# Decay and beta rows of a delta rule: by DMA broadcast from memory instead of by products with one-hot columns

## The chip, the cores and the metric

The kernel runs on one core of one Trainium2 chip. The metric is the time of one execution in device microseconds. Engines go by the names of the profile: PE (matrix products), DVE (vector), ACT (scalar, activations), POOL (GpSimd), SP (here only the issue of transfers). SBUF is the on-chip working memory of 128 partitions, PSUM the memory in eight banks that products are written to.

## The reference, cut to what matters

The program is two blocks, float32, for 512 tokens of width 1024. The first is a gated linear attention block with a routed mixture of experts. The second has a gated delta rule layer, a feed-forward layer, an attention layer and another feed-forward layer. The change lies in the gated delta rule, which for 8 heads of 128 computes

```
g_cum = cumsum(g within a chunk);  decay = exp(g_cum[i] - g_cum[j]) for i >= j
a_low = strict_lower((k*beta) @ k^T * decay)
[u, w] = solve(I + a_low, [v*beta, k*beta*exp(g_cum)])
attn  = (q @ k^T) * decay;   q_decay = q * exp(g_cum);   k_decay = k * exp(g_last - g_cum)
```

The kernel uses chunks of 128 tokens, so a head has four tiles of 128x128.

## The kernel before, in words

Stages follow each other, each in a block with a barrier of all engines at its end: the first block and its experts, then the projection stage of the delta rule, then the stage that inverts `I + a_low` (the one that changes), then the pass over the chunks with the output projection, a feed-forward, attention and a feed-forward.

In the projection stage ACT and DVE make `rows`, 8 partitions (one a head) by 4 rows of 512: row 0 is the decay's running sum, row 1 beta, row 2 a product of both, row 3 scratch. The same figures turned into columns are `gcols`.

The inverting stage goes over the heads in four pairs p (NPAIR), the two heads of a pair being u = 0 and 1. It needs row 0 and row 1 of each head repeated on all 128 partitions. `spread_rows` gets them by matrix products: the stationary operand is one column of the 8x8 identity repeated 128 times, the moving operand is `rows`, so that each product has 8 rows of contraction and 512 columns. The results are in PSUM banks 4u and 4u+1. From them:

- DVE `difference`: dm = (row 0 spread) - (column of the same), then the minimum of dm and 0
- ACT `exps`: er = exp(row 0 spread), then dm = exp(dm)
- DVE `decays`: dm times the triangular mask, then aT2 = (beta spread) * dm
- PE `pair_products` into the same two banks, once all of that has read them: K with K, Q with K; DVE `read_products` multiplies them by dm and aT2; `first_level` sets up the inverse tT2; `turn_t` and `turn_kv` transpose, ACT copies, DVE `keep_kd`.

Then a pair goes through six levels (LEVELS) of doubling. In each, POOL `mask` makes bmT from aT2, PE `level` multiplies it (L2006), ACT `keep_m` copies the result, PE multiplies twice more (L2006), and DVE `update` corrects tn and tT (L2238, L2240). After the sixth, `finish` applies the inverse.

Each engine's order is written out by hand: the preparation of pair p+1 stands at set places between the levels of pair p. On PE these are level 1: spread_rows, 3: pair_products, 4: turn_t, 5: turn_kv. On ACT 2: exps, 5: keep_t, 6: keep_kv. On DVE the differences stand ahead of the updates of level 2, `decays` behind the updates of levels 2 and 3, products and the first head's `first_level` ahead of the updates of level 4. Pair 0 has nothing beside it: its preparation is done in a row before the first level.

Weights come through `ring`, eight slots that SP fills (L203). In the inverting stage SP has no work.

Of the kernel before, what the change touches and what calls it, by code (L numbers as in the profile page):

```python
# [13 lines left out]
F32 = mybir.dt.float32  # L14
U8 = mybir.dt.uint8
F32R = mybir.dt.float32r
ALU = mybir.AluOpType
ACT = mybir.ActivationFunctionType
AX = mybir.AxisListType
P = 128  # L20
# [111 lines left out]
def program(nc, xT, ctxT, stream, experts, small, params, heads8, wdec, table, windows, outT):  # L132
    with ExitStack() as ctx:
# [13 lines left out]
        def sem(name):  # L147

            live.append(nc.alloc_semaphore(name))
            return live[-1]  # L150

        def kept_sem(name):
            return ctx.enter_context(nc.semaphore(name))
# [18 lines left out]

        h2_dram = nc.dram_tensor("h2_dram", (T, D), F32).ap()
        y_dram = nc.dram_tensor("y_dram", (2 * T, D), F32).ap()
        h_stored = kept_sem("h_stored")

        ident = tab[:, TABLES["ident"]]
# [185 lines left out]
        with nc.Block() as block:  # L363
            @block.sync
            def _(sp):
                load_blocks(sp, STREAM["out"].start + SLOTS)
# [1192 lines left out]
        rows = tab[0:8, TABLES["rcount"]].rearrange("p (a t) -> p a t", a=4)  # L1559
        ea = sb("ea", [8, 1], on=gdn)  # L1560
        ab_done, ab_act, ab_dve, ab_tr, ab_cols = (sem(n) for n in ("ab_done", "ab_act", "ab_dve", "ab_tr", "ab_cols"))
        st = gdn.enter_context(ExitStack())
        g_hi = sb("g_hi", [P, KT, T], F32R, on=st)
        g_lo = over("g_lo", [P, KT, T], F32R, "hn")
# [27 lines left out]
        with nc.Block() as block:  # L1592
# [144 lines left out]
            def _(act):  # L1737
# [48 lines left out]
                def step(ins):  # L1786
                    made[0] += 1
                    ins.then_inc(ab_act, 1)
                    act.wait_ge(ab_act, made[0])
# [4 lines left out]
                step(act.activation(rows[:, 3, :], rows[:, 3, :], ACT.Exp, scale=-1.0))  # L1794
                step(act.activation(rows[:, 3, :], rows[:, 3, :], ACT.Ln, bias=1.0))
                act.wait_ge(ab_dve, 5)
                step(act.activation(rows[:, 3, :], rows[:, 0, :], ACT.Exp))

                def roots(u, before):
# [162 lines left out]
        def tiles(x):  # L1962
            return x.rearrange("p (n i) -> p n i", n=TT)

        def every_tile(mask):
# [7 lines left out]
        tn2, tT2 = (sb(f"inv_{n}", [P, 2, 2, TT * H], on=st) for n in ("tn", "tT"))  # L1973
        er = sb("inv_er", [P, 2, T], on=st)
        whole = sml[:, 0:2 * T].rearrange("p (u t) -> p u t", u=2)
        names = ("spread", "diff", "expd", "exprow", "beta", "paired", "dve", "qdec", "t_tr", "kv_tr",
                 "t_copy", "kd_ready", "kv_ready", "masked", "m_done", "m_copy", "xy_done", "tn_up", "tT_up", "fin_done",
                 "fin_kept")
        S = {n: [sem(f"i_{n}{u}") for u in range(2)] for n in names}
# [10 lines left out]
        def off_block(x, rows):  # L1990
            return x[H * rows:H * rows + H, :].rearrange("p (n i) -> p n i", n=TT)[:, :, H:P]
        with nc.Block() as block:
            @block.tensor
            def _(pe):
                def four(out, lhsT, rhs):
# [11 lines left out]
                                          rhs[:, own if wide_rhs else near], start=True, stop=True)  # L2007
                    return m

                def spread_rows(p, u):  # L2010
                    h = 2 * p + u
                    if p:
                        pe.wait_ge(S["kd_ready"][u], p)
                        pe.wait_ge(S["kv_ready"][u], 2 * TT * p)
                    for a in range(2):
                        m = pe.matmul(ps[:, 4 * u + a, :], tab[0:8, h:h + 1].to_broadcast([8, P]), rows[:, a, :],
                                      start=True, stop=True)
                    m.then_inc(S["spread"][u], 1)

                def pair_products(p, u):  # L2020
                    h = 2 * p + u
                    pe.wait_ge(S["diff"][u], 2 * p + 1)
                    pe.wait_ge(S["exprow"][u], p + 1)
                    pe.wait_ge(S["beta"][u], p + 1)
                    four(ps[:, 4 * u, :], K[:, h, :], K[:, h, :])
                    four(ps[:, 4 * u + 1, :], K[:, h, :], Q[:, h, :]).then_inc(S["paired"][u], 1)

# [51 lines left out]
                    four(ps[:, 4 * u + 2, :], whole[:, u, :], V[:, h, :])  # L2079
                    four(ps[:, 4 * u + 3, :], K[:, h, :], whole[:, u, :]).then_inc(S["fin_done"][u], 1)  # L2080
                both = range(2)
                for part in (spread_rows, pair_products, turn_t, turn_kv):
                    for u in both:
                        part(0, u)
                for p in range(NPAIR):
                    beside = {1: spread_rows, 3: pair_products, 4: turn_t, 5: turn_kv} if p + 1 < NPAIR else {}
                    for lv in range(1, LEVELS + 1):
                        level(p, lv)
                        if lv in beside:
                            for u in both:  # L2090
                                beside[lv](p + 1, u)
                    for u in both:
                        finish(p, u)

            @block.scalar
            def _(act):
                def exps(p, u):
                    act.wait_ge(S["spread"][u], p + 1)
                    if p:
                        act.wait_ge(S["qdec"][u], p)  # L2100
                        act.wait_ge(S["dve"][u], DVES * p)
                    act.wait_ge(S["diff"][u], 2 * p + 1)
                    act.activation(er[:, u, :], ps[:, 4 * u, :], ACT.Exp).then_inc(S["exprow"][u], 1)
                    act.wait_ge(S["diff"][u], 2 * p + 2)
                    act.activation(dm[:, u, :], dm[:, u, :], ACT.Exp).then_inc(S["expd"][u], 1)

# [23 lines left out]
                def keep_result(p, u):  # L2130
                    h = 2 * p + u
                    act.wait_ge(S["fin_done"][u], p + 1)
                    for n, keep in enumerate((V, K)):
                        act.activation(keep[:, h, :], ps[:, 4 * u + 2 + n, :], ACT.Copy).then_inc(S["fin_kept"][u], 1)
                for part in (exps, keep_t, keep_kv):
                    for u in range(2):
                        part(0, u)
                for p in range(NPAIR):
                    beside = {2: exps, 5: keep_t, 6: keep_kv} if p + 1 < NPAIR else {}
                    for lv in range(1, LEVELS + 1):  # L2140
                        for u in range(2):
                            keep_m(p, lv, u)
                        if lv in beside:
                            for u in range(2):
                                beside[lv](p + 1, u)
                    for u in range(2):
                        keep_result(p, u)
# [32 lines left out]
            def _(ve):  # L2180
                def bycol(a, h):
                    return gcols[:, a, :, h:h + 1].to_broadcast([P, TT, P])

                def difference(p, u):
                    ve.wait_ge(S["spread"][u], p + 1)
                    ve.tensor_tensor(tiles(dm[:, u, :]), tiles(ps[:, 4 * u, :]), bycol(0, 2 * p + u), ALU.subtract
                                     ).then_inc(S["diff"][u], 1)
                    ve.wait_ge(S["diff"][u], 2 * p + 1)
                    ve.tensor_scalar(dm[:, u, :], dm[:, u, :], 0.0, None, ALU.min).then_inc(S["diff"][u], 1)

                def decays(p, u):
                    d = tiles(dm[:, u, :])
                    ve.wait_ge(S["expd"][u], p + 1)
                    ve.tensor_tensor(d, d, every_tile(tab[:, TABLES["incl"]]), ALU.mult).then_inc(S["dve"][u], 1)
                    ve.wait_ge(S["dve"][u], DVES * p + 1)
                    ve.tensor_tensor(aT2[p % 2][:, u, :], ps[:, 4 * u + 1, :], dm[:, u, :], ALU.mult
                                     ).then_inc(S["beta"][u], 1)

                def read_products(p, u):
# [887 lines left out]
```

## Time and profile before

| | |
|---|---|
| median of 3 runs | 2266.87 us |
| lowest and highest | 2261.90 and 2267.45 us |
| span of the profiled execution | 2263.8 us |
| mean granted TensorE clock | 0.939 of full speed |
| the inverting stage | from about 955.4 to 1131 us |

The profiled execution has no time of its own listed beside its span; the span lies within the three runs. The profile gives each instruction's place in that one execution, in microseconds from its start. The granted clock is the share of full speed at which PE was let run: 1.00 is 2.4 GHz, 0.50 is 1.2 GHz. A line number is that of the kernel; L2016 is the product of `spread_rows`, L1998 the product of `pair_products` (and of `finish`). PE counts each float32 product twice in the number of instructions.

### The profile page before, as it was taken

What the parts mean: (1) busy time and instruction counts of PE and PEld (TensorE: products, weight loads), DVE (VectorE), ACT (ScalarE), POOL (GpSimd) and SP (SyncE); (2) the same over time, 40 slices, a digit from 0 to 9 for tenths busy, and PEclk for the clock granted to TensorE, in tenths of its full rate; (3) what the DMA queues carried; (4) which work ended last, traced back from release to release, by engine and by line L of the source; (5) the groups of instructions that cost most, each with busy time, mean ns of one, the idle gap of its engine ahead of it and who ended that gap; (6) DMA issues with size and microseconds to landing.
All of it is one profiled execution on the core that took longest, in us unless ns stands there. A gap on an engine that the chain in (4) does not pass through costs nothing. (4 is left out here: it accounts for less than half of the span.)

```text
span 2263.8 us, 28841 instructions
## 1 busy us (share of the span) xinstructions
PE 2018.8 (89%) x11286; PEld 1512.0 (67%) x11286; DVE 994.9 (44%) x1397; ACT 688.1 (30%) x1078; POOL 321.3 (14%) x254
## 2 busy tenths in 40 slices
PE   5988884978785999678889999999999889999999
PEld 2756663322225777467887888888777677888887
DVE  3440444111115567855553444433488434434433
ACT  2432132111103445324432322222443543222222
POOL 1332010111113343033420100000100001000000
PEclk9999897999998999879989999999999889999999
DMA  8137016899981122100002222222222012222221
GB/s 340 47 131 269 12 63 252 330 423 425 423 344 76 68 91 84 56 2 2 3 10 78 100 93 93 102 93 103 77 82 75 10 38 84 93 102 93 96 100 47
DMA packets 61949, 283.32 MB, mean 125 GB/s; under 512 B 9984, under 2 KB 11296, under 8 KB 52512
## 3 DMA queue, kind: packets, MB, share of 16 engines
q1 hardware_dynamic: 53072, 266.95, 31.3%
q0 software_dynamic: 6256, 11.03, 1.3%
q10 hardware_dynamic: 2528, 4.01, 0.5%
q8 instruction: 69, 1.13, 0.2%
q14 instruction: 24, 0.20, 0.0%
HBM read 280.90 MB, written 14.68 MB: 131 GB/s over the span
## 5 line engine op out<-in xcount | busy, mean ns | idle before, releaser
L307 PE MATMUL ps<-ff_hhi,ff_whi 128*128 128x512 f32 x704 | 276.8, 393 | 8.6 <-DVE ff_hlo L2662 8.3
L308 PE MATMUL ps<-ff_hhi,ff_wlo 128*128 128x512 f32 x704 | 275.4, 391 | 0.0
L309 PE MATMUL ps<-ff_hlo,ff_whi 128*128 128x512 f32 x704 | 275.3, 391 | 0.0
L2580 DVE TENSOR_TENSOR ff_wlo<-ring,ff_whi 128x1024 fp32r<-128x1024 f32 x132 | 163.4, 1238 | 247.3 <-ACT ff_whi L2576 247.3
L2576 ACT ACTIVATE ff_whi<-ring 128x1024 fp32r<-128x1024 f32 x132 | 139.3, 1055 | 321.3 <-PE ps L309 299.7
L1451 PE MATMUL ps<-w_up,hgT 128*64 128x512 f32 x576 | 144.6, 654 | 45.8 <-DMA w_up<-experts 45.8
L307 PEld LDWEIGHTS ps<-ff_hhi,ff_whi 128*128 128x128 f32 x704 | 133.2, 189 | 38.5 <-DVE ff_wlo L2580 10.2
L309 PEld LDWEIGHTS ps<-ff_hlo,ff_whi 128*128 128x128 f32 x704 | 133.0, 189 | 28.0
L308 PEld LDWEIGHTS ps<-ff_hhi,ff_wlo 128*128 128x128 f32 x704 | 133.1, 189 | 27.7 <-issue 0.5
L307 PE MATMUL ps<-ff_ahi,ff_whi 128*128 128x512 f32 x352 | 136.9, 389 | 0.0
L308 PE MATMUL ps<-ff_ahi,ff_wlo 128*128 128x512 f32 x352 | 136.9, 389 | 0.0
L309 PE MATMUL ps<-ff_alo,ff_whi 128*128 128x512 f32 x352 | 136.9, 389 | 0.0
L1451 PEld LDWEIGHTS ps<-w_up,hgT 128*64 128x64 f32 x576 | 44.3, 150 | 133.9 <-issue 105.9
L307 PE MATMUL ps<-g_hi,g_w 128*128 128x512 f32 x256 | 103.2, 403 | 0.0
L309 PE MATMUL ps<-g_lo,g_w 128*128 128x512 f32 x256 | 102.2, 399 | 0.0
L308 PE MATMUL ps<-g_hi,ring_lo 128*128 128x512 f32 x256 | 100.3, 392 | 0.0
L1721 POOL TENSOR_TENSOR ring_lo<-ring,g_w 128x1024 fp32r<-128x1024 f32 x32 | 77.6, 2433 | 118.5 <-ACT g_w L1741 118.5
L2599 ACT ACTIVATE hctx<-hctx 128x512 f32<-128x512 f32 x44 | 27.8, 632 | 200.1 <-DVE hctx L2641 200.1
L309 PEld LDWEIGHTS ps<-ff_alo,ff_whi 128*128 128x128 f32 x352 | 66.1, 188 | 13.8
L308 PEld LDWEIGHTS ps<-ff_ahi,ff_wlo 128*128 128x128 f32 x352 | 66.1, 188 | 13.8
L307 PEld LDWEIGHTS ps<-ff_ahi,ff_whi 128*128 128x128 f32 x352 | 66.1, 188 | 13.5
L2641 DVE TENSOR_TENSOR hctx<-ps,ff_rs 128x512 f32<-128x512 f32 x44 | 30.4, 690 | 96.7 <-PE ps L309 96.7
(553 smaller groups left out, 3862.0 us busy)
## 6 DMA issues: line engine op xcount, KB each, us to landing
ring<-stream SPq DMA_DIRECT2D x276, 512.0 KB, 3.2
w_up<-experts SPq DMA_DIRECT2D x36, 2048.0 KB, 17.0
mix<-experts SPq DMA_DIRECT2D x18, 1024.0 KB, 20.8
hn<-experts SPq DMA_DIRECT2D x18, 1024.0 KB
yrow<-y_dram SPq DMA_DIRECT2D x4, 1024.0 KB, 8.0
tab<-table POOLq DMA_DIRECT2D x1, 2528.5 KB, 12.3
res<-xT ACTq DMA_DIRECT2D x1, 2048.0 KB
h_dram<-mix SPq DMA_DIRECT2D x4, 512.0 KB, 11.3
```

The source lines that it names most:

```text
L307: pe.matmul(out, w_hi, a_hi, start=start, stop=False)
L308: pe.matmul(out, w_lo, a_hi, start=False, stop=False)
L309: return pe.matmul(out, w_hi, a_lo, start=False, stop=stop)
L1451: m = pe.matmul(ps[half[u], s, :], hgT[:, s, k, half[u]], w_up[:, s, u, k * 512:(k + 1) * 512], start=k == 0, stop=k == KT - 1)
L1721: pool.tensor_tensor(ring_lo[:, s, :], ring[:, s, :], g_w[:, n % 4, :].bitcast(F32), ALU.subtract).then_inc(w_split, 1)
L2576: act.activation(w_hi[:, j % 2, :], ring[:, s, :], ACT.Copy).then_inc(w_rounded, 1)
L2580: ve.tensor_tensor(w_lo[:, j % 2, :], ring[:, (B0 + j) % SLOTS, :], w_hi[:, j % 2, :].bitcast(F32), ALU.subtract).then_inc(blocks_done, 1)
L2599: act.activation(sg[:, p % 4, :], sg[:, p % 4, :], ACT.Silu).then_inc(silu_done, 1)
L2641: ve.tensor_tensor(sg[:, p % 4, :], ps[:, 2 * (p % 4), :], rs[:, :], ALU.mult).then_inc(g_scaled, 1)
```

## The change

The two rows go to memory once and come back on all partitions by DMA.

- In the projection stage ACT issues one transfer of rows 0 and 1 of all heads to `rows_dram` (32 KB), between two of its steps.
- In the inverting stage SP issues for each pair two transfers of row 0 (one a head, 512 numbers read onto each of 128 partitions, 256 KB written) into dm, and two of row 1 into aT2. For pairs after the first the transfers into dm wait for `keep_kd` of the pair before (semaphore kd_ready) and its `dve` steps, those into aT2, from the third pair on, for the last mask of two pairs before.
- `spread_rows` is gone from PE: 16 products. `pair_products` no longer waits for the readers of the spread rows, only, from the second pair on, for the pair before.
- ACT makes er in a part of its own, `exp_rows`, from dm in SBUF; it stands one level earlier (1), `exps` of dm stays at level 2.
- DVE `difference` reads dm and writes dm, after er has been made; the beta product reads aT2 and writes aT2. Before, one operand of each was in PSUM.

```
+        rows_dram = nc.dram_tensor("rows_dram", (2, HEADS, T), F32).ap()
...
                 act.wait_ge(ab_dve, 5)
+                act.dma_start(rows_dram.rearrange("a h t -> h a t"), rows[:, 0:2, :]).then_inc(rows_out, 16)
                 step(act.activation(rows[:, 3, :], rows[:, 0, :], ACT.Exp))
...
+            @block.sync
+            def _(sp):
+                def all_rows(a, h):
+                    return rows_dram[a, h:h + 1, :].to_broadcast([P, T])
+                sp.wait_ge(rows_out, 16)
+                for p in range(NPAIR):
+                    for u in range(2):
+                        h = 2 * p + u
+                        if p:
+                            sp.wait_ge(S["kd_ready"][u], p)
+                            sp.wait_ge(S["dve"][u], DVES * p)
+                        sp.dma_start(dm[:, u, :], all_rows(0, h)).then_inc(S["g_in"][u], 16)
+                    for u in range(2):
+                        h = 2 * p + u
+                        if p >= 2:
+                            sp.wait_ge(S["masked"][u], LEVELS * (p - 1))
+                        sp.dma_start(aT2[p % 2][:, u, :], all_rows(1, h)).then_inc(S["beta_in"][u], 16)
...
-                def spread_rows(p, u):
+                def pair_products(p, u):
                     h = 2 * p + u
                     if p:
                         pe.wait_ge(S["kd_ready"][u], p)
                         pe.wait_ge(S["kv_ready"][u], 2 * TT * p)
-                    for a in range(2):
-                        m = pe.matmul(ps[:, 4 * u + a, :], tab[0:8, h:h + 1].to_broadcast([8, P]), rows[:, a, :],
-                                      start=True, stop=True)
-                    m.then_inc(S["spread"][u], 1)
-
-                def pair_products(p, u):
-                    h = 2 * p + u
-                    pe.wait_ge(S["diff"][u], 2 * p + 1)
-                    pe.wait_ge(S["exprow"][u], p + 1)
-                    pe.wait_ge(S["beta"][u], p + 1)
...
-                    beside = {1: spread_rows, 3: pair_products, 4: turn_t, 5: turn_kv} if p + 1 < NPAIR else {}
+                    beside = {3: pair_products, 4: turn_t, 5: turn_kv} if p + 1 < NPAIR else {}
...
-                def exps(p, u):
-                    act.wait_ge(S["spread"][u], p + 1)
+                def exp_rows(p, u):
+                    act.wait_ge(S["g_in"][u], 16 * (p + 1))
...
-                    act.wait_ge(S["diff"][u], 2 * p + 1)
-                    act.activation(er[:, u, :], ps[:, 4 * u, :], ACT.Exp).then_inc(S["exprow"][u], 1)
+                    act.activation(er[:, u, :], dm[:, u, :], ACT.Exp).then_inc(S["exprow"][u], 1)
+
+                def exps(p, u):
...
-                    beside = {2: exps, 5: keep_t, 6: keep_kv} if p + 1 < NPAIR else {}
+                    beside = {1: exp_rows, 2: exps, 5: keep_t, 6: keep_kv} if p + 1 < NPAIR else {}
...
-                    ve.wait_ge(S["spread"][u], p + 1)
-                    ve.tensor_tensor(tiles(dm[:, u, :]), tiles(ps[:, 4 * u, :]), bycol(0, 2 * p + u), ALU.subtract
+                    ve.wait_ge(S["exprow"][u], p + 1)
+                    ve.tensor_tensor(tiles(dm[:, u, :]), tiles(dm[:, u, :]), bycol(0, 2 * p + u), ALU.subtract
...
-                    ve.tensor_tensor(aT2[p % 2][:, u, :], ps[:, 4 * u + 1, :], dm[:, u, :], ALU.mult
+                    ve.wait_ge(S["beta_in"][u], 16 * (p + 1))
+                    ve.tensor_tensor(aT2[p % 2][:, u, :], aT2[p % 2][:, u, :], dm[:, u, :], ALU.mult
```

## Rows read from the trace of the kernel before

**Rows 1.** The page: busy time of the engines over the whole span.

```profile
PE 2018.8 (89%) x11286; PEld 1512.0 (67%) x11286; DVE 994.9 (44%) x1397; ACT 688.1 (30%) x1078; POOL 321.3 (14%) x254
```

**Rows 2.** Windows: length, busy PE, PEld, DVE, ACT, POOL, granted clock, DMA share, GB/s.

```profile
1034.70:1041.20 6.50, 6.47 (x96) 5.06 (x96) 1.96 (x5) 3.63 (x8) 2.14 (x2) 0.50 0.01 3
1107.00:1127.00 20.00, 18.22 (x512) 16.87 (x512) 8.78 (x23) 9.12 (x24) 10.69 (x10) 1.00 0.02 3
```

**Rows 3.** Timeline of pair 0's preparation: start, length, what.

```profile
955.44 7.16 PE L2016 MATMUL ps<-tab 8*128 8x512 f32 x8 [17.53 <-PEq L1592]
959.30 0.69 DVE L2186 TENSOR_TENSOR inv_dm<-ps,gcols 128x512 f32<-128x512 f32 x1 [1.63 <-PE ps L2016]
960.08 1.28 ACT L2103 ACT_TABLE_LOAD   x1 [12.47 <-DVE inv_dm L2186]
965.26 2.05 PE L1998 MATMUL ps<-K 128*128 128x128 f32 x8 [2.66 <-DVE inv_aT L2196]
972.41 1.64 DVE L2213 TENSOR_TENSOR inv_tT<-inv_aT,tab 64x256 f32<-64x256 f32 x2
```

**Rows 4.** Timeline of DVE: first update of levels 1, 2, 4 of pairs 0 to 2; 1, 2 of pair 3.

```profile
988.81 0.42 DVE L2238 TENSOR_TENSOR inv_tn<-inv_tn,ps 128x256 f32<-128x256 f32 x1 [4.57 <-PE ps L2006]
...
998.28 0.42 DVE L2238 TENSOR_TENSOR inv_tn<-inv_tn,ps 128x256 f32<-128x256 f32 x1 [2.77 <-PE ps L2006]
...
1010.62 0.42 DVE L2238 TENSOR_TENSOR inv_tn<-inv_tn,ps 128x256 f32<-128x256 f32 x1 [0.47 <-PE ps L2006]
...
1030.76 0.42 DVE L2238 TENSOR_TENSOR inv_tn<-inv_tn,ps 128x256 f32<-128x256 f32 x1 [6.34 <-PE ps L2006]
...
1039.95 0.42 DVE L2238 TENSOR_TENSOR inv_tn<-inv_tn,ps 128x256 f32<-128x256 f32 x1 [2.76 <-PE ps L2006]
...
1051.98 0.42 DVE L2238 TENSOR_TENSOR inv_tn<-inv_tn,ps 128x256 f32<-128x256 f32 x1 [0.47 <-PE ps L2006]
...
1071.10 0.42 DVE L2238 TENSOR_TENSOR inv_tn<-inv_tn,ps 128x256 f32<-128x256 f32 x1 [6.34 <-PE ps L2006]
...
1079.39 0.42 DVE L2238 TENSOR_TENSOR inv_tn<-inv_tn,ps 128x256 f32<-128x256 f32 x1 [2.48 <-PE ps L2006]
...
1090.72 0.42 DVE L2238 TENSOR_TENSOR inv_tn<-inv_tn,ps 128x256 f32<-128x256 f32 x1 [0.47 <-PE ps L2006]
...
1109.85 0.42 DVE L2238 TENSOR_TENSOR inv_tn<-inv_tn,ps 128x256 f32<-128x256 f32 x1 [6.34 <-PE ps L2006]
...
1113.32 0.42 DVE L2238 TENSOR_TENSOR inv_tn<-inv_tn,ps 128x256 f32<-128x256 f32 x1 [1.75 <-PE ps L2006]
```

**Rows 5.** Timeline of PE: spread products beside level 1 of pairs 1 and 2.

```profile
1031.62 4.38 PE L2016 MATMUL ps<-tab 8*128 8x512 f32 x8
...
1071.96 3.77 PE L2016 MATMUL ps<-tab 8*128 8x512 f32 x8
```

**Rows 6.** One line's instructions (min/median/max ns) and, last, POOL's mask in pair 3.

```profile
L2194 DVE TENSOR_TENSOR inv_dm<-inv_dm,tab x8: 681/685/1489, 963.7 to 1084.4; 128x512 f32<-128x512 f32 x8
L2196 DVE TENSOR_TENSOR inv_aT<-ps,inv_dm x4: 690/690/692, 964.4 to 1046.4; 128x512 f32<-128x512 f32 x4
L2163 POOL TENSOR_TENSOR inv_bmT<-inv_aT,tab x24: 1088/1094/1552, 970.4 to 1096.5; 128x512 f32<-128x512 f32 x24
1111.33 2.14 POOL L2163 TENSOR_TENSOR inv_bmT<-hctx,tab 128x512 f32<-128x512 f32 x2 [1.33 <-PE ps L2006]
```

**Rows 7.** The page: transfers by line, KB each, median us from issue to landing.

```profile
ring<-stream SPq DMA_DIRECT2D x276, 512.0 KB, 3.2
...
yrow<-y_dram SPq DMA_DIRECT2D x4, 1024.0 KB, 8.0
...
outT<-res SPq DMA_DIRECT2D x8, 256.0 KB, 2.1
```

**Rows 8.** Timeline: the last KD of pair 1 (DVE), then the last copy of its level 1 (ACT).

```profile
1023.75 0.67 DVE L2226 TENSOR_TENSOR KD<-ps,inv_dm 128x512 f32<-128x512 f32 x1
...
1029.70 0.78 ACT L2127 ACTIVATE inv_m<-ps 64x256 f32<-64x256 f32 x2 [0.19 <-PE ps L2006]
```

More of the change, by code:

```diff
@@ L1561, in program @@
         ab_done, ab_act, ab_dve, ab_tr, ab_cols = (sem(n) for n in ("ab_done", "ab_act", "ab_dve", "ab_tr", "ab_cols"))
+        rows_out = sem("rows_out")
         st = gdn.enter_context(ExitStack())
@@ L1975, in program @@
         whole = sml[:, 0:2 * T].rearrange("p (u t) -> p u t", u=2)
-        names = ("spread", "diff", "expd", "exprow", "beta", "paired", "dve", "qdec", "t_tr", "kv_tr",
+        names = ("g_in", "beta_in", "diff", "expd", "exprow", "beta", "paired", "dve", "qdec", "t_tr", "kv_tr",
                  "t_copy", "kd_ready", "kv_ready", "masked", "m_done", "m_copy", "xy_done", "tn_up", "tT_up", "fin_done",
@@ L2081, in _ @@
                 both = range(2)
-                for part in (spread_rows, pair_products, turn_t, turn_kv):
+                for part in (pair_products, turn_t, turn_kv):
                     for u in both:
@@ L2134, in keep_result @@
                         act.activation(keep[:, h, :], ps[:, 4 * u + 2 + n, :], ACT.Copy).then_inc(S["fin_kept"][u], 1)
-                for part in (exps, keep_t, keep_kv):
+                for part in (exp_rows, exps, keep_t, keep_kv):
                     for u in range(2):
```

## The prediction

> **What bounds the kernel now.** I read the page first, for where PE is short of work, then the stage's timeline engine by engine, then windows for the granted clock, then single lines and the transfers.
>
> PE is busy 89% of the span [rows 1]. A busy share this high can still hide waits, since products are pipelined and half-speed products count as busy too. So the question is what sets the pace inside the inverting stage. Its engines run in a ring: mask, product, copy, two products, update. A level ends with the updates of DVE, so I measure it from first update to first update. Pair 3 has nothing beside its levels, and there a level takes 1113.32 - 1109.85 = 3.47 us [rows 4]. That is the ring's own pace at full clock [rows 2].
>
> Pairs 0, 1 and 2 have spread products, differences and exponentials between the updates of level 1 and those of level 2, and the distance is 998.28 - 988.81 = 9.47, 1039.95 - 1030.76 = 9.19 and 1079.39 - 1071.10 = 8.29 us [rows 4]. So what stands there costs 5 to 6 us a pair, although the spread products themselves take 4.38 and 3.77 us [rows 5]. The rest is clock: in the 6.5 us behind 1034.70 the granted clock is 0.50, the lower level, with PE busy 6.47 us of them [rows 2]. The fall comes 3.1 us after the first of the spread products [rows 2, 5], which use 8 of 128 rows, and without an idle PE. Pair 3, with no spread products, stays at 1.00 over 20 us, though PE is less busy there (18.22 us of 20) [rows 2].
>
> In pair 0's preparation everything is a chain with nothing beside it: spread products from 955.44, the first difference at 959.30, pair products from 965.26, `first_level` at 972.41 [rows 3].
>
> **Term 1, the preparation of pair 0.** Before, 972.41 - 955.4 = 17.0 us from the stage's start to `first_level`. After, PE has its pair products at once: 8 instructions took 2.05 us at most at the low clock [rows 3], there are 32, so they are done within 8.2 us, by 963.6. The other chain starts with a transfer. A 256 KB one landed in 2.1 us and a 512 KB one in 3.2 [rows 7]. The nearest in size is a store, the nearest in direction is the larger, so I take 2.7: 955.5 + 2.7 = 958.2. Then ACT's table load of 1.28 us [rows 3], which stood behind its wait before and will again, and the first exponential, which I set at 0.6 (about what a difference takes, 0.69 [rows 3]): 960.1. From there DVE does two differences with their minima, two masks and two beta products, four products with what PE made. A 128x512 operation takes 0.69 [rows 3, 6]; with minima a little shorter I count 1.15 for a difference, 1.4 for a head's `decays`, 1.3 for its `read_products`, in all 2 x 3.85 = 7.7. `first_level` then starts at 967.8 instead of 972.4: **4.6 us gained**. The bounds: 5.2 with a landing of 2.1, 4.1 with 3.2. If the broadcast lands like the 1024 KB transfers, in 8.0 [rows 7] (four broadcasts are issued together, 1024 KB in sum), the term is -0.7, a loss. I take 4.6, since DVE needs only the first one to begin, and beta some 5 us later.
>
> **Term 2, level 1 to level 2 of pairs 0 to 2.** The spread products leave PE's queue: level 2's first product need not wait for them, and the reason for the slow clock goes. PE would then be ready as in pair 3, 3.47 us after the first update. What comes last now is DVE, which still has both differences ahead of the level's updates. Four updates end about 1.7 us after the first begins, two differences with minima take 2.3: 4.0 us is the lower bound. The upper bound comes from what the change adds. The difference used to read PSUM and now reads both operands from SBUF, as the mask product L2194 always did. That one takes 0.685 us in the median but up to 1.489, the beta product with one operand in PSUM never over 0.692, and POOL's masks reach 1.552 from 1.09 [rows 6]. Two SBUF operands thus run into POOL, at 0.8 us a time. POOL's masks for the next level start 1111.33 - 1109.85 = 1.48 us after the first update and last 2.14 [rows 4, 6], which is right under the differences. With two such hits it is 5.6. I take one and a half, 5.2, for pairs 1 and 2, and 6.0 for pair 0, where PE runs at half clock until about 990. Gain: 9.47 - 6.0 = 3.5, 9.19 - 5.2 = 4.0, 8.29 - 5.2 = 3.1, **in sum 10.6 us**. Bounds: 14.2 with no hit (distances of 4.8, 4.0 and 4.0), 9.4 with two each (6.4, 5.6, 5.6).
>
> [...]
>
> **Term 3, level 2 to level 4.** Before 12.34, 12.03 and 11.33 us [rows 4]. The first two still had part of the slow clock. Here DVE is nearly full with `decays`, products and `first_level`, and PE's wait for the beta product goes away, but the beta product may now meet POOL itself. I take 11.5 for all three: gains of 0.8, 0.5 and -0.2, **in sum 1.1 us** (bounds -1 and 2.5).
>
> **What costs nothing.** ACT issues the store of rows in the projection stage while PE has blocks of work ahead. If that cover were gone, it would cost an issue, well under 1 us. Four SP transfers a pair stand on a queue that is otherwise empty. The one into dm of pair 2's second head is issued when the KD at 1023.75 is done, at 1024.4, and ACT can use it after its copy at 1029.70, at 1030.5 [rows 8]; ACT must be back for level 2's copies about 1.7 us later. So a landing within about 6 us is hidden for every pair, and then `keep_m` of level 2 waits behind it on ACT, and PE for that. `exp_rows` itself (1.1 us for two heads) fills time in which ACT waits for PE. Beta has a level more. The 256 KB copies are small beside what the queues carry elsewhere.
>
> **Sum.** 4.6 + 10.6 + 1.1 = 16.3 us. The stages behind start earlier by it, since their weights come through a ring that is full. From the profiled span of 2263.8 that gives 2247.5. The span lies 3.1 us under the median of 2266.87, and I apply the difference to the median: 2250.6.
>
> **The rivals.**
> (a) More is gained: no port hits, clock at full from 990 on, landing at 2.1 us. 5.2 + 14.2 + 2.5 = 21.9, giving 2245. For it: L2194 was hit only in part of its 8 cases [rows 6]. Against: the overlap in time is plain. The Trainium skill (TensorE: Matmul & The Clock Gate, What's actually happening) has the gate follow how busy the engine was, with nothing on how many rows a product uses. By that the falls would stay, as PE is as busy after the change as before it, and (a) would be out; the trace speaks against the page, 0.50 with PE busy 6.47 of 6.50 us.
> (b) Less is gained: each broadcast lands late, at 5 us, because 128 copies come from one 2 KB piece of memory, and each level 1 to 2 has two port hits: 2.3 + 9.4 + 0 = 11.7, giving 2255; at 6 to 7 us of landing 8 to 10 us are left.
> (c) The transfer takes the place of the product and nothing is left to measure: landing time L is exposed as L - 2.7 in pair 0, L - 6 in each of the three others, so 16.3 is used up at 4L - 20.7 = 16.3, L = 9.2 us. Somewhat above the 8.0 of a 1024 KB transfer, for a quarter of the bytes. 2267.
> (d) Slower: the same mechanism past L = 9.2, which is where it decides; at 12 us the sum is 27.3 - 16.3 = 11 us lost, 2278. The profile has nothing like it for 256 KB on an idle set of queues (2.1 us [rows 7]); a pathological reading of one place is the only ground.
>
> **How the numbers follow.** Forecast (13 to 19 us gained) 0.53, (a) 0.20, (b) 0.15, (c) 0.07, (d) 0.05. A measurement here tells 0.3%, 6.8 us. The forecast, (a) and (b) are beyond it: faster 0.88, within 0.07, slower 0.05. The range 2243 to 2260 takes in (a) with its bound and (b) down to 7 us of gain; the three runs of before lie up to 5.5 us apart, which is some of its width. The likeliest case alone is 2247 to 2254.
>
> **What would show it.** Pair 0's `first_level` starts near 12.4 us after the stage's start. The distance from first update of level 1 to that of level 2 is 5 to 6 us in pairs 0 to 2, and what ends DVE's idle time there is nothing: its own queue is last. The difference shows a maximum near 1.5 us beside a minimum of 0.69. The granted clock stays at 1.00 through the level 1 to 2 stretches of pairs 1 and 2. ACT's `exp_rows` waits for DMA in pair 0 alone. The prediction is wrong if exp_rows waits for DMA in each pair, if the clock falls in the same places without the products, or if DVE's slower operations lengthen levels 2 to 4 by more than a microsecond.

## The result, and the profile after

The median of 20 runs is 2249.84 us after the change and 2269.41 us before it, 19.6 us less. The ratio over all runs is 0.993, that is 15.9 us, with a 95% interval of 0.9912 to 0.9948, that is 12 to 20 us. The profiled execution has a span of 2243.0 us where the one of before had 2263.8.

After the change the times come in two groups some 17 us apart (12 runs from 2244.67 to 2253.09, 8 from 2261.14 to 2266.95), before it they spread from 2261.90 to 2283.53 without so clear a gap, so a median also depends on how many of its runs are of which kind. In the profiled executions the difference stands ahead of the stage that was changed, which starts 954 to 963 us into some kernels and 972 to 975 us into others. I therefore also give the length of the stage by itself, from its first operation on DVE (the memset of inv_m) to the first update of pair 3. It is 1109.85 - 955.68 = 154.2 us before [rows 4] and 1091.27 - 954.97 = 136.3 us after, 17.9 us less. A second profile of after gives 136.0. Of the 20.8 us by which the two profiled spans differ, 0.7 stand ahead of the stage, 17.9 are this length, and 2.2 come behind the first update of pair 3, where I did not look.

The page of after, beside [rows 1]: PE is busy for 30 us less and DVE for 9 us more. PE's figure holds more than the 16 products, since a product at the lower clock counts for longer: in dead8, below, 16 of L2027 take 1.07 us at 0.50 and 0.64 at 1.00.

```profile
PE 1988.5 (89%) x11254; PEld 1495.0 (67%) x11254; DVE 1004.1 (45%) x1397; ACT 689.5 (31%) x1078; POOL 324.6 (14%) x254
```

The timeline of after for pair 0's preparation, one engine after the other, beside [rows 3]:

```profile
954.67 0.81 SPq L2007 DMA_DIRECT2D inv_dm<-rows_dram  x2
...
954.73 2.05 PE L2019 MATMUL ps<-K 128*128 128x128 f32 x8 [17.53 <-PEq L1594]
...
954.69 1.28 ACT L2113 ACT_TABLE_LOAD   x1 [7.80 <-PEq L1594]
958.64 1.29 ACT L2113 ACTIVATE inv_er<-inv_dm 128x512 f32<-128x512 f32 x2 [2.67 <-DMA inv_dm<-rows_dram]
...
959.38 0.69 DVE L2198 TENSOR_TENSOR inv_dm<-inv_dm,gcols 128x512 f32<-128x512 f32 x1 [2.42 <-ACT inv_er L2113]
...
966.56 1.64 DVE L2226 TENSOR_TENSOR inv_tT<-inv_aT,tab 64x256 f32<-64x256 f32 x2
```

PE begins with the pair products. ACT waits 2.67 us for the transfer, but only after its table load is done: that load no longer stands in the chain. `first_level` starts 11.6 us behind the memset of 954.97; before it was 972.41 - 955.68 = 16.7.

The updates of DVE, beside [rows 4]: first of level 1 and of level 2 for pairs 0, 1 and 2, then pair 3's level 1.

```profile
982.17 0.42 DVE L2251 TENSOR_TENSOR inv_tn<-inv_tn,ps 128x256 f32<-128x256 f32 x1 [3.70 <-PE ps L2027]
...
987.47 0.41 DVE L2251 TENSOR_TENSOR inv_tn<-inv_tn,ps 128x256 f32<-128x256 f32 x1
...
1018.93 0.42 DVE L2251 TENSOR_TENSOR inv_tn<-inv_tn,ps 128x256 f32<-128x256 f32 x1 [6.36 <-PE ps L2027]
...
1024.27 0.41 DVE L2251 TENSOR_TENSOR inv_tn<-inv_tn,ps 128x256 f32<-128x256 f32 x1
...
1054.57 0.42 DVE L2251 TENSOR_TENSOR inv_tn<-inv_tn,ps 128x256 f32<-128x256 f32 x1 [6.37 <-PE ps L2027]
...
1059.91 0.41 DVE L2251 TENSOR_TENSOR inv_tn<-inv_tn,ps 128x256 f32<-128x256 f32 x1
...
1091.27 0.42 DVE L2251 TENSOR_TENSOR inv_tn<-inv_tn,ps 128x256 f32<-128x256 f32 x1 [6.36 <-PE ps L2027]
```

The distances are 5.30, 5.34 and 5.34 us, from 9.47, 9.19 and 8.29. The rows at level 2 have no bracket: DVE had not been idle. Its own queue is what comes last. This is that queue in pair 1 with POOL's masks beside it:

```profile
1020.57 1.48 DVE L2198 TENSOR_TENSOR inv_dm<-inv_dm,gcols 128x512 f32<-128x512 f32 x1
1022.09 1.20 DVE L2201 TENSOR_SCALAR inv_dm<-inv_dm 128x512 f32<-128x512 f32 x1
1023.21 0.68 DVE L2198 TENSOR_TENSOR inv_dm<-inv_dm,gcols 128x512 f32<-128x512 f32 x1
1023.93 0.43 DVE L2201 TENSOR_SCALAR inv_dm<-inv_dm 128x512 f32<-128x512 f32 x1
...
1020.42 2.59 POOL L2175 TENSOR_TENSOR inv_bmT<-hctx,tab 128x512 f32<-128x512 f32 x2 [1.33 <-PE ps L2027]
```

The same two operations take 1.48 and 1.20 us while POOL works and 0.68 and 0.43 when it has ended. Pairs 0 and 2 have the same pattern (1.49 and 1.20, 1.48 and 1.20). I call such a lengthening a hit. The first of the two is on a difference, with both inputs in SBUF, the second on a minimum, which has one. And the granted clock in that stretch, beside [rows 2], is full:

```profile
1018.50:1027.50 9.00, 7.05 (x212) 6.48 (x210) 8.24 (x14) 5.59 (x13) 5.08 (x5) 1.00 0.01 4
```

### The profile page after: what moved, and what is told of

Read it like the earlier page. It is cut to its first block and busy times, and to the rows that moved or that the text cites. A ratio compares the mean times of both kernels' runs of the same rounds, so it can differ in the third digit from the quotient of the medians.

```text
span 2243.0 us, 28792 instructions
## 1 busy us (share of the span) xinstructions
PE 1988.5 (89%) x11254; PEld 1495.0 (67%) x11254; DVE 1004.1 (45%) x1397; ACT 689.5 (31%) x1078; POOL 324.6 (14%) x254
## 5 line engine op out<-in xcount | busy, mean ns | idle before, releaser
L308 PEld LDWEIGHTS ps<-ff_hhi,ff_whi 128*128 128x128 f32 x704 | 132.9, 189 | 38.1 <-DVE ff_wlo L2593 10.2
L310 PEld LDWEIGHTS ps<-ff_hlo,ff_whi 128*128 128x128 f32 x704 | 132.9, 189 | 27.8
## 6 DMA issues: line engine op xcount, KB each, us to landing
w_up<-experts SPq DMA_DIRECT2D x36, 2048.0 KB, 17.7
mix<-experts SPq DMA_DIRECT2D x18, 1024.0 KB, 20.8
hn<-experts SPq DMA_DIRECT2D x18, 1024.0 KB, 21.9
```

The source lines that it names most:

```text
L308: pe.matmul(out, w_hi, a_hi, start=start, stop=False)
L310: return pe.matmul(out, w_hi, a_lo, start=False, stop=stop)
```

## The experiments

All lengths of the stage are taken as above. The four distances of a pair are those from first update to first update of neighbouring levels. In after they are 5.3, 3.4, 8.0 to 8.1 and 6.4 to 7.5 us, in before 8.3 to 9.5, 3.7 to 4.5, 7.6 to 7.9 and 6.7 to 7.8.

The fourth distance has to be read with the granted clock beside it. In each pair of after PE is idle for 2.6 us there, until `first_level` is done. Windows of after, with the columns of [rows 2], two in pair 1 and two in pair 2, one in the idle time and one behind it:

```profile
1037.00:1038.00 1.00, 0.00 (x0) 0.00 (x0) 0.94 (x5) 0.00 (x0) 0.00 (x0) 1.00 0.00 0
1039.00:1040.00 1.00, 1.00 (x36) 1.00 (x38) 0.00 (x0) 0.00 (x0) 0.00 (x0) 1.00 0.00 0
...
1073.00:1074.00 1.00, 0.00 (x0) 0.00 (x0) 0.94 (x4) 0.00 (x0) 0.00 (x0) 1.00 0.00 0
1075.00:1076.00 1.00, 1.00 (x25) 1.00 (x24) 0.00 (x0) 0.00 (x0) 0.00 (x0) 0.50 0.00 0
```

In pair 1 the clock stays at 1.00 and level 4 to 5 takes 6.45 us. In pair 2, behind the same idle time, it is at 0.50 for about 3 us and the level takes 7.52, in pair 0 likewise 7.40. Such a fall costs 0.8 to 1.1 us (after and fused_diff have 6.4 to 6.5 without one and 7.3 to 7.5 with one). Why it comes behind one idle time and not behind the same in the next pair is open. Since a stage can hold none to three of them, a difference of a microsecond or two between two stages is not by itself the work of an edit.

| kernel | stage us | level 1-2 | 2-3 | 3-4 | 4-5 | median of all runs |
|---|---|---|---|---|---|---|
| before | 154.2 | 9.5, 9.2, 8.3 | 4.5, 4.4, 3.7 | 7.9, 7.6, 7.6 | 7.75, 6.72, 6.72 | 2269.41 |
| after | 136.3 | 5.3, 5.3, 5.3 | 3.4, 3.4, 3.4 | 8.1, 8.0, 8.0 | 7.40, 6.45, 7.52 | 2249.84 |
| dead8 | 156.9 | 8.9, 8.8, 9.2 | 5.4, 4.5, 5.3 | 9.6, 8.1, 9.6 | 7.79, 7.50, 7.69 | 2269.01 |
| dead128 | 150.6 | 7.2, 7.3, 7.3 | 4.5, 4.5, 4.5 | 9.6, 9.6, 9.6 | 7.44, 7.32, 7.26 | 2266.52 |
| early_diff | 139.3 | 5.3, 3.5, 3.5 | 3.4, 4.5, 4.5 | 8.0, 9.6, 9.6 | 7.26, 8.06, 7.83 | 2249.78 |
| fused_diff | 133.4 | 4.8, 4.8, 4.8 | 3.4, 3.4, 3.4 | 8.0, 8.0, 8.0 | 6.44, 7.26, 6.44 | 2241.67 |
| early_fused | 139.1 | 4.8, 3.5, 3.5 | 3.4, 4.5, 4.5 | 8.0, 9.6, 9.6 | 6.44, 8.09, 8.08 | 2251.92 |
| write_only_masks | 129.7 | 4.0, 4.1, 4.1 | 3.3, 3.3, 3.3 | 7.4, 7.4, 7.3 | 6.72, 6.73, 7.76 | 2237.25, one run |
| late_exp_rows | 139.5 | 5.8, 5.9, 5.9 | 4.1, 4.2, 4.1 | 8.6, 8.6, 8.6 | 6.44, 6.45, 6.45 | 2265.45, one run |
| landing_twice | 146.5 | 8.5, 5.3, 5.4 | 4.6, 3.4, 3.4 | 8.1, 8.0, 8.0 | 7.42, 6.44, 7.52 | 2274.89, one run |
| mask_on_pool | 136.2 | 4.8, 4.8, 4.8 | 3.3, 3.3, 3.3 | 8.1, 8.1, 8.1 | 7.82, 7.00, 8.07 | 2247.79 |

**dead8: the spread products back, read by nobody.**

```
+                def dead_products(p, u):
+                    h = 2 * p + u
+                    pe.wait_ge(S["kd_ready"][u], p)
+                    pe.wait_ge(S["kv_ready"][u], 2 * TT * p)
+                    for a in range(2):
+                        pe.matmul(ps[:, 4 * u + a, :], tab[0:8, h:h + 1].to_broadcast([8, P]), rows[:, a, :], start=True, stop=True)
...
-                    beside = {3: pair_products, ...
+                    beside = {1: dead_products, 3: pair_products, ...
```

> After plus the spread products at their old place beside level 1 of pairs 0 to 2, of 8 rows as they were, read by nobody (dead). My theory: two costs come back, 3.4 us of PE and the clock that falls behind products of few rows. The distance from first update of level 1 to level 2 goes from 5.3 us to 8 or more in at least two of the three pairs, with a granted clock of 0.50 for some us behind the products; the stage is 7 to 11 us longer than in after. Rival one, the clock follows nothing but how busy PE is: the clock stays at 1.00 there and the distance is 3.4 + 3.5 = 6.9, the stage 4.8 us longer. Rival two, the cost was DVE's wait for the products, not PE: distance stays at 5.3 to 5.5.

Nobody reads them, and yet level 1 to 2 is at 8.8 to 9.2 us again. Two rows of DVE (its timeline, pair 2) and two windows, one from the update on and over the products, one behind them:

```profile
1075.73 0.42 DVE L2258 TENSOR_TENSOR inv_tn<-inv_tn,ps 128x256 f32<-128x256 f32 x1 [6.37 <-PE ps L2027]
...
1084.91 0.42 DVE L2258 TENSOR_TENSOR inv_tn<-inv_tn,ps 128x256 f32<-128x256 f32 x1 [5.32 <-PE ps L2027]
```

```profile
1075.70:1080.00 4.30, 4.30 (x40) 2.22 (x37) 3.56 (x8) 0.93 (x2) 0.20 (x1) 0.94 0.01 2
1080.00:1086.00 6.00, 5.97 (x92) 4.90 (x92) 0.75 (x2) 2.67 (x6) 2.14 (x2) 0.50 0.01 3
```

DVE now sits idle for 5.32 us until PE is done, and PE runs at the lower clock, 1.2 GHz, with 5.97 us busy of 6. The fall is there in all three pairs. The theory holds for this distance. Rival one, a clock that stays at 1.00 and 6.9 us, falls, and so does rival two, that only DVE's wait for the products had cost time. My figure for the stage was too small: it is 20.6 us longer than after, not 7 to 11. Level 1 to 2 accounts for 11.0 of it. Levels 2 to 4 account for 8.1, which I had not expected: DVE's operations with two SBUF inputs are hit there as in the next run, and the low clock still holds when the updates of level 2 begin. The remaining 1.5 stand behind level 4.

**dead128: the same with all 128 rows.**

```
-                        pe.matmul(ps[:, 4 * u + a, :], tab[0:8, h:h + 1].to_broadcast([8, P]), rows[:, a, :], start=True, stop=True)
+                        pe.matmul(ps[:, 4 * u + a, :], ident, K[:, h, :], start=True, stop=True)
```

> As dead8, but the dead products use all 128 rows (stationary the identity, moving K of the same head), with the same 512 columns and the same count. My theory: PE's 3.4 us come back, the clock does not fall, distance 6.9 us in the three pairs, stage about 5 us longer than after. Rival, any such run of wide float32 products at that place lets the clock fall, whatever its rows: same as dead8, 8 us or more and 0.50 behind them.

Timeline of DVE in pair 2, then a window from the first dead product on:

```profile
1082.22 0.42 DVE L2258 TENSOR_TENSOR inv_tn<-inv_tn,ps 128x256 f32<-128x256 f32 x1 [6.36 <-PE ps L2027]
...
1089.47 0.42 DVE L2258 TENSOR_TENSOR inv_tn<-inv_tn,ps 128x256 f32<-128x256 f32 x1 [3.40 <-PE ps L2027]
...
1091.07 1.48 DVE L2213 TENSOR_TENSOR inv_dm<-inv_dm,tab 128x512 f32<-128x512 f32 x1
1092.59 1.47 DVE L2216 TENSOR_TENSOR hctx<-hctx,inv_dm 128x512 f32<-128x512 f32 x1
```

```profile
1082.00:1098.00 16.00, 15.39 (x286) 12.56 (x284) 11.80 (x23) 5.30 (x12) 5.14 (x5) 1.00 0.01 3
```

7.25 us and a clock of 1.00. So the place, the number and the width of the products cost 7.25 - 3.47 = 3.8 us in each pair against a ring with nothing beside it, and 1.9 against the 5.3 of after, where DVE is last. Behind the 8-row products another 1.6 to 1.9 us are lost by the clock. Ahead of the fall PE is busy all the time in both kernels (4.30 of 4.30 us in dead8's window, 1.00 in each microsecond from 1001 to 1005 in dead128), so its busy time does not tell the two apart. The two kernels also differ in the data of both operands (a one-hot column with the rows of decay and beta, against the identity with K); that the data's values matter was not tried. Here DVE's mask and beta products take 1.48 and 1.47 us, and level 2 to 3 is at 4.5. The stage is 14.3 us longer than after, not 5: 5.7 at level 1 to 2 and 8.0 in levels 2 to 4, where DVE's operations are hit more often than in after.

**early_diff: the differences leave DVE's queue between level 1 and 2.**

```
+                        sp.dma_start(er[:, u, :], all_rows(0, 2 * p + u)).then_inc(S["er_in"][u], 16)
...
-                    ve.wait_ge(S["exprow"][u], p + 1)
+                    ve.wait_ge(S["g_in"][u], 16 * (p + 1))
...
-                        if more and lv == 2:
+                        if more and lv == (1 if p else 2):
                             difference(p + 1, 0)
```

> After, with row 0 sent by DMA into dm and also into er, so that the difference waits for its transfer and not for the exponential; for the pairs prepared beside pairs 1 and 2 both differences go ahead of the updates of level 1, where DVE idles 6.4 us. My theory, DVE with its two differences is what sets level 1 to 2: the distance falls from 5.34 to 3.5 to 3.9 us for pairs 1 and 2 and stays at 5.3 for pair 0; pair 0's first_level starts about 1.4 us earlier; the stage is 4 to 5.5 us shorter, time about 2245 where after gives 2250. Rival one, PE or ACT sets that distance: it stays at 5.0 to 5.4 and only pair 0's 1.4 us are gained. Rival two, the differences hit POOL's mask and delay the updates of level 1: the distance from level 4 to the next level 1 grows by as much as is gained, time as after.

In pairs 1 and 2 level 1 to 2 falls to 3.48 and 3.47 us, the ring's own pace: DVE was the bound there, and rival one, PE or ACT, falls. Pair 0's `first_level` comes 0.5 us earlier (11.1 us behind the memset), not 1.4. And the stage is 3.0 us longer than in after, where I had given 4 to 5.5 us less. None of my cases had that. The 3.7 us gained are given back, 5.3 at level 2 to 3 and 3 to 4 and 1.8 at level 4 to 5, where PE's idle time is longer and the clock lower. At levels 2 to 4 DVE's operations with two SBUF operands now meet POOL's masks. Timeline of DVE, then POOL, pair 1:

```profile
1023.36 1.48 DVE L2210 TENSOR_TENSOR inv_dm<-inv_dm,tab 128x512 f32<-128x512 f32 x1
1024.87 1.47 DVE L2213 TENSOR_TENSOR inv_aT<-inv_aT,inv_dm 128x512 f32<-128x512 f32 x1
...
1030.22 1.70 DVE L2230 TENSOR_TENSOR inv_tT<-inv_aT,tab 64x256 f32<-64x256 f32 x2
1031.95 0.95 DVE L2234 COPY egl<-inv_er 128x4 f32<-128x4 f32 x1
1032.82 1.81 DVE L2239 TENSOR_TENSOR inv_tT<-tab,inv_tT 64x256 f32<-64x256 f32 x2
...
1023.20 2.59 POOL L2179 TENSOR_TENSOR inv_bmT<-hctx,tab 128x512 f32<-128x512 f32 x2 [1.30 <-PE ps L2031]
1030.55 2.33 POOL L2179 TENSOR_TENSOR inv_bmT<-hctx,tab 128x512 f32<-128x512 f32 x2 [4.76 <-PE ps L2031]
```

The three operations of `first_level` take 0.87, 0.17 and 0.86 us in the same pair of before; here 1.70, 0.95 and 1.81, and the level 9.6 us. In after the mask comes later against DVE, and only the last of the three is hit.

**fused_diff: difference and minimum in one.**

```
-                    ve.tensor_tensor(tiles(dm[:, u, :]), tiles(dm[:, u, :]), bycol(0, 2 * p + u), ALU.subtract ...
-                    ve.tensor_scalar(dm[:, u, :], dm[:, u, :], 0.0, None, ALU.min) ...
+                    for n in range(TT):
+                        c = slice(n * P, (n + 1) * P)
+                        ve.tensor_scalar(dm[:, u, c], dm[:, u, c], gcols[:, 0, n, 2 * p + u:2 * p + u + 1], 0.0,
+                                         ALU.subtract, ALU.min).then_inc(S["diff"][u], 1)
```

> After, with the difference and the minimum made in one operation a tile (128 columns, the column as scalar operand) in place of two over 512 columns: one SBUF tensor as input. My theory, port hits of two-input and fast-mode operations are 1.9 of the 5.34 us: the small operations take about 0.2 us each, 1.7 us for both heads, and meet POOL less; distance 4.2 to 4.8 us, stage 2 to 3.5 us shorter. Rival, they lose as much in 8 fixed costs or are hit as before (single operations over 0.8 us): distance 5.2 or more.

The eight small operations together, and their line:

```profile
1035.90 3.25 DVE L2200 TENSOR_SCALAR inv_dm<-inv_dm,gcols 128x128 f32<-128x128 f32 x8
```

```profile
L2200 DVE TENSOR_SCALAR inv_dm<-inv_dm,gcols x32: 271/275/1135, 975.7 to 1075.0; 128x128 f32<-128x128 f32 x32
```

4.8 us against 5.3, at the upper edge of what I expected; the stage is 2.9 us shorter. Of these 1.6 are level 1 to 2; 1.2 are level 4 to 5, where the clock fell in one pair and in after in two, and this part I can't put down to the edit. One input does not protect them: the longest took 1.135 us, the median 0.275. They still win, as 3.25 us stand in place of 3.8. Timed again beside after:

> After, unchanged, timed again on the chip of the two below. The stage should be 136.3 us from its first memset to the first update of pair 3, as before; the whole time 2245 to 2266, since the part ahead of the stage takes 955 us or 972 us by its own clock and not by the change.

> fused_diff unchanged, timed again. Stage 133.4 us, 2.9 us shorter than after; lowest of the whole times 2 to 4 us under the lowest of after_again, medians too noisy to tell.

Stages of 136.0 and 132.9 us; medians of 2248.89 (11 runs) and 2244.50 (6 runs), lowest times 2242.74 and 2240.81. The ratios to before are 0.9918 (0.9886 to 0.995) and 0.9882 (0.9845 to 0.9919): the intervals overlap, so the gain over after is not shown by the whole time. The stage is 3 us shorter in both pairs of profiles, but again with one fall of the clock at level 4 to 5 against two; level 1 to 2 gives 1.6 us both times, and that much is shown.

**write_only_masks: POOL reads nothing.** The masks of levels 2 to 6 are left out and replaced by memsets.

```
-                    pool.tensor_tensor(tiles(bmT[:, u, :]), tiles(aT2[p % 2][:, u, :]), every_tile(tab[:, m0:m0 + P]), ...
+                    pool.memset(bmT[:, u, :], 0.0).then_inc(S["masked"][u], 1)
```

> After, with POOL's masks of levels 2 to 6 replaced by memsets of bmT: POOL then only writes SBUF and reads nothing. It leaves out the masking, so that the corrections of levels 2 to 6 are zero. My theory, DVE operations with two SBUF inputs lose their 0.8 us to POOL's reads: the difference, the beta product and the set-up of first_level fall to their undisturbed 0.69, 0.69 and 0.87 us everywhere, level 1 to 2 to 4.0 to 4.3 us, level 3 to 4 from 8.0 to 7.6 or less. The minimum, a one-input operation that is hit too in after (1.20 against 0.43 us), may still be hit by a write. Rival: the extension is DVE's own wait for something else (its exponential, the transfer): the long ones stay at 1.48.

One line's instructions, the difference and then the minimum:

```profile
L2201 DVE TENSOR_TENSOR inv_dm<-inv_dm,gcols x8: 673/684/692, 958.4 to 1051.9; 128x512 f32<-128x512 f32 x8
...
L2204 DVE TENSOR_SCALAR inv_dm<-inv_dm x8: 426/428/730, 959.1 to 1052.6; 128x512 f32<-128x512 f32 x8
```

The difference is never longer than 0.692 us; the minimum, with one input, is still hit, once in each pair (0.730). Level 1 to 2 is 4.06 us, and the stage 6.6 us shorter than after. So POOL's masks cost 1.3 us at level 1 to 2 and 0.7 at level 3 to 4 of each pair after the change, over what the memsets still cost; without the 0.3 us by which the minimum is still hit, level 1 to 2 would be at 3.8. The memsets are also shorter than the masks (0.525 against 1.09 us), so a part of the gain is POOL being busy for less, which the run does not tell apart from its not reading.

**late_exp_rows: the move of exp_rows undone.**

```
-                    beside = {1: exp_rows, 2: exps, 5: keep_t, 6: keep_kv}
+                    beside = {2: both_exps, 5: keep_t, 6: keep_kv}
```

> After with one part undone: exp_rows goes back from level 1 to level 2, ahead of exps, behind the copies of level 2 on ACT. Theory: the differences on DVE wait for it and the updates of level 2 stand behind the differences, so level 1 to 2 grows from 5.34 to 6.0 to 6.8 us for pairs 0 to 2, stage 2 to 4 us longer. Rival: the place of exp_rows is of no account, since the differences were held by POOL anyway: distance at most 5.6.

5.8 to 5.9 us, a little under what I gave, because the differences now come after POOL's masks and are no longer hit. What is held back appears behind it, in levels 2 to 4 (4.1 and 8.6). Up to level 4 the three pairs take 5.4 us more than in after: the move to level 1 is worth that. The stage is only 3.2 us longer, since the clock did not fall at level 4 to 5 in any pair (6.44 to 6.45 us), which gave 2.0 back.

**landing_twice: each row into dm is sent twice, one after the other.**

```
+                        sp.dma_start(dm[:, u, :], all_rows(0, h)).then_inc(S["g_pre"][u], 16)
+                        sp.wait_ge(S["g_pre"][u], 16 * (p + 1))
                         sp.dma_start(dm[:, u, :], all_rows(0, h)).then_inc(S["g_in"][u], 16)
```

> After, with each transfer of row 0 into dm made twice, the second waiting for the first, so that a row lands some 3.5 us later. Theory: pair 0 pays it in full (first_level 3 to 4 us later than after, which has 11.6 us from the stage's first memset), the three other pairs hide it (distance level 1 to 2 stays within 0.5 us of 5.34). Rival, the transfers are on the path in each pair: each distance grows by 2 us or more.

`first_level` starts 17.5 us after the memset instead of 11.6, 5.9 us later and not 3 to 4, since the second head's pair of transfers stands behind the first's on SP's queue. For pairs 2 and 3 ACT waits 1.0 and 0.6 us and the distance does not grow (5.33 and 5.37 us), for pair 1 it does: 8.5 us. ACT's timeline shows its two waits, beside pair 0's levels:

```profile
1009.19 0.63 ACT L2115 ACTIVATE inv_er<-inv_dm 128x512 f32<-128x512 f32 x1 [1.41 <-DMA inv_dm<-rows_dram]
1013.22 0.63 ACT L2115 ACTIVATE inv_er<-inv_dm 128x512 f32<-128x512 f32 x1 [3.40 <-DMA inv_dm<-rows_dram]
```

So the cover that the prediction gave as about 6 us for every pair is smaller for the pair prepared beside pair 0, where `keep_kd` and the first level lie close together: in after its first transfer is issued at 976.79 and ACT is free for it at 981.7, 4.9 us later. For the pair prepared beside pair 1 it is 9.1 us for the first head (1009.58 to 1018.68) and 6.1 for the second.

**early_fused and mask_on_pool: two attempts to go further.** The first is the two edits above together. The second takes the triangular mask off DVE:

```
-                    ve.tensor_tensor(d, d, every_tile(tab[:, TABLES["incl"]]), ALU.mult).then_inc(S["dve"][u], 1)
+                    ve.nop().then_inc(S["dve"][u], 1)
...
+                    pool.tensor_tensor(tiles(AT[:, h, :]), tiles(AT[:, h, :]), every_tile(tab[:, TABLES["incl"]]), ALU.mult)
```

> early_diff and fused_diff together. early_diff had level 1 to 2 at 3.48 us but level 2 to 3 at 4.5 and 3 to 4 at 9.6, fused_diff 4.8, 3.43 and 8.0. Theory, the differences no longer matter once they are early, what then comes last are the mask product, beta product and first_level against POOL's masks: 3.5, 4.5, 9.6 again, stage within 1 us of early_diff's 139.3 and longer than fused_diff's 133.4. Rival, the gains add up: stage near 131.

> fused_diff, and the triangular mask taken off DVE: dm stays unmasked, and POOL masks the Q-K products in SBUF (AT) behind decay_q, one 128x512 operation of 1.1 us a head. Theory, DVE's queue is what sets level 2 to 3 (3.43 with the hits) and 3 to 4 (8.0): pair 0's first_level comes 1.4 us earlier, level 3 to 4 falls by 0.7 us in each of three pairs, stage 129.5 to 131 us. Rival, POOL's added reads hit first_level and keep_kd or delay its own masks: levels 4 to 6 grow by what is gained and the stage stays at 133 or more.

early_fused is 3.5, 4.5 and 9.6 us again, 139.1: removing DVE's work at level 1 to 2 does not add up. mask_on_pool brings `first_level` of pair 0 1.1 to 1.6 us earlier (10.0 us behind the memset), but the first update comes no earlier (27.1 us behind the memset in both), level 3 to 4 stays at 8.1, 4 to 5 grows to 7.8, 7.0 and 8.1, and the stage ends 3 us behind fused_diff. At full clock the fourth distance is 7.00 against 6.44, which is 0.6 us a pair by POOL's added work; the rest of the growth, about 1 us, is one more fall of the clock. The time of the stage is what its rival had said, its cause is shown for the first part only. Of all kernels here fused_diff has the shortest stage that computes everything.

## Why the prediction was right

**The size.** 16.3 us were forecast, 2250.6 us; the median is 2249.84, the ratio gives 15.9, the stage 17.9. That the median is met within a microsecond is luck: the forecast stood on a median of before of 2266.87 (3 runs), which is 2269.41 over 20, and the medians differ by 19.6 us. What holds is that the stage gains what was added up, in the places where it was said, and two of the terms came out by errors that cancel.

**Term 1, 4.6 us forecast, 5.1 measured** (16.7 to 11.6). Two steps in it were wrong and cancelled, which is luck. The first broadcast took 4.0 us from its issue at 954.67 to ACT's start at 958.64, not 2.7; the transfers from and to rows_dram took 3.0 to 4.6 us to land, with a median of 3.5. And the table load of 1.28 us, of which I wrote that it "stood behind its wait before and will again", now runs at 954.69, ahead of the wait. The order of DVE's twelve operations and their sum, 7.7 us, came out at 7.2.

**Term 2, 10.6 us forecast, 11.0 measured.** Forecast distances 6.0, 5.2 and 5.2, measured 5.30, 5.34 and 5.34. One and a half hits of 0.8 us on a bound of 4.0 were taken; there are two in every pair, of 0.79 and 0.77 us, on a bound of 3.8 (the differences begin 1.64 us behind the first update, and two of them with their minima take 2.13 in late_exp_rows, where nothing hits them). 5.2 and 5.3 agree because the two errors cancel. The term also had its hits on the differences, by the reading that two SBUF inputs meet POOL; the second one fell on a minimum, with one. Pair 0 was given 0.8 us for a low clock that it did not have: the clock is at 1.00 from 980 until behind level 4. early_diff (3.5 us with the differences gone) and write_only_masks (4.06 with POOL's masks not in the way) show that DVE's queue and POOL make up this distance, as the term says. dead8 and dead128 show what the products had cost over that, 1.9 us by their time on PE and 1.6 to 1.9 by the clock.

**The clock.** The prediction set the row against the Trainium skill (TensorE: Matmul & The Clock Gate, What's actually happening), which ties the gate to how busy the engine is. That alone does not account for what is measured here: with PE busy all the time over the products in both kernels, the clock is at 0.50 behind products of 8 rows (5.97 of 6.00 us busy) and at 1.00 behind the same number of 128 rows. The measurement decides. As said, the two kernels differ in the operands' data too.

**Ports.** The rule of the Trainium skill (SBUF — State Buffer, Who interferes with whom), two SBUF inputs against a GpSimd read, agrees with L2198 (1.48 against 0.68 us) and with write_only_masks (0.692 at most). For operations with one input the same section of the Trainium skill makes an exception of the fast modes, which tensor_scalar can enter. The minimum is a tensor_scalar, and it took 1.20 us against 0.43: the trace agrees. The prediction had reckoned with two SBUF inputs alone.

**Term 3, 1.1 us forecast, 1.3 measured.** Level 2 to 4 takes 11.5, 11.4 and 11.4 us; 11.5 was given for all.

**What was not in it.** 0.8 us between `first_level` and the first update of pair 0 (16.4 to 15.6), where the clock rises at 979 instead of 990. Against it, 0.8 us more at level 4 to 5 of pair 2 (6.72 to 7.52), where the clock now falls behind an idle PE and before did not; pairs 0 and 1 gain 0.35 and 0.27 there. Issues of ACT and SP cost nothing that shows; ACT's store took 0.53 us.

**The rivals.** (a), 21.9 us, failed at the hits. (b) had both causes right and their sizes too large: two hits in each pair, but 11.0 us gained and not 9.4, and broadcasts slower than thought, at 3.5 us and not 5. Its 8 to 10 us for a landing of 6 to 7 do not follow from its own terms, which give 10.7 to 6.7. (c) and (d) did not come about. landing_twice shows that their mechanism is real: the stage loses 10.2 us of its 18, 5.9 in pair 0's preparation and 4.4 in levels 1 to 3 of pair 0, none beside pairs 1 and 2. (c) had spread the loss over all pairs. In landing_twice the first head's row lands 6 to 7 us and the second's 10 to 11 us behind the first issue, so it does not measure the landing at which the gain is used up.

**The signs.** `first_level` came at 11.6 us behind the start of the stage (12.4 was said), the distances at 5.3 with DVE's own queue last, the longest difference at 1.49 us beside 0.68, the clock at 1.00 through level 1 to 2 of all pairs, and ACT's `exp_rows` waited for DMA once, in pair 0. None of the signs of being wrong showed.

## What to carry to other kernels

A product with few rows is not a cheap way to repeat a row: four products of 8 rows and 512 columns took 3.8 to 4.4 us on PE where four of 128 rows took 3.7, and in this kernel the clock was at the lower level behind those of 8 rows. When its result moves from PSUM to SBUF, look at each reader on DVE whose second operand is in SBUF too, and at what POOL does at that moment. Where two engines meet at a port, a saving at one place shifts the meeting to the next: three edits that relieved DVE at one place (early_diff, early_fused, mask_on_pool) gave a longer stage than fused_diff, and only the length of the whole stage says which edit pays. That length in turn has to be compared with the granted clock of each stretch beside it, as two equal idle times of PE can end at either level.

## What the runs showed of the hardware that I had not expected

The granted clock behind 8-row products, 0.50 for some 6 us with PE busy all the time, and 1.00 behind 128-row products of the same number and width.

The fall to 0.50 behind an idle time of 2.6 us of PE, in pairs 0 and 2 of after and not in pair 1.

A one-input DVE operation of 128x512 (minimum) goes from 0.43 to 1.20 us beside a POOL operation, one of 128x128 from 0.275 to 1.135, and still 0.730 where POOL only writes.

The time ahead of the stage comes in two sizes. These two windows, of after and of dead128, lie in the first block, far ahead of everything that was edited:

```profile
200.00:300.00 100.00, 86.51 (x717) 65.94 (x716) 42.85 (x93) 21.96 (x37) 7.03 (x5) 0.86 0.22 77
```

```profile
200.00:300.00 100.00, 89.74 (x654) 69.75 (x653) 29.41 (x72) 15.62 (x25) 5.19 (x3) 0.71 0.21 73
```

At 0.71 against 0.86 less work is done in the same 100 us, and the stage begins 17.7 us later (972.70 and 954.97). In all thirteen profiles the two go together: where the stage begins at 972 us or later (five) the clock of this window is 0.69 to 0.74, in the eight others 0.86 to 0.88. What decides between the two is open; it was not looked into.
